# Reordering weight splits, activations and waits at the stage boundaries of a two-block fp32 kernel

## The reference

```python
h = h + jnp.concatenate([hm, ha], axis=-1) @ w_out[l]
h = h + memory_cross_attention(rmsnorm(h, g_cross[l]), rmsnorm(mem, g_mem[l]), ...)
h = h + peer_ffn(rmsnorm(h, g_ffn[l]), w_pq[l], ...)
```

## Time and profile before

| | |
|---|---|
| median of three executions | 1679.29 us (1677.75 to 1684.41) |
| profiled execution, its own time | 1677.7 us |
| its span, first to last instruction | 1675.9 us |
| busy: PE, DVE, ACT, POOL | 1652.3, 1237.3, 934.3, 237.0 us |
| DMA | 323.40 MB, mean 193 GB/s |

### The profile page before, as it was taken

The page is one execution under the profiler, slowest core; times in us unless marked ns, Lnnn a source line. Parts: engine busy times, 40 slices in busy tenths (PEclk is TensorE's granted clock), DMA queues, the critical chain, the costliest instruction groups (busy, mean ns, idle before and its releaser), DMA issues.

```text
span 1675.9 us, 30270 instructions
## 1 busy us (share of the span) xinstructions
PE 1652.3 (99%) x12006; PEld 1540.9 (92%) x12006; DVE 1237.3 (74%) x1894; ACT 934.3 (56%) x1138; POOL 237.0 (14%) x329
## 2 busy tenths in 40 slices
PE   8999999999999999999999999999999999999999
PEld 8899999999999999988888888999999888899987
DVE  6775467999998666666766767787799555769974
ACT  7875565545555555554554554786555357555542
POOL 0000000003757767301101000000000000000000
PEclk9999999999999999999999999999999999999999
DMA  8345244776555555777777776633555544345553
GB/s 303 129 158 190 103 179 139 227 235 216 186 177 189 189 189 189 270 238 241 237 243 237 240 244 220 232 127 126 184 198 198 190 163 151 126 152 202 202 186 116
DMA packets 73948, 323.40 MB, mean 193 GB/s; under 512 B 8679, under 2 KB 8935, under 8 KB 55888
## 3 DMA queue, kind: packets, MB, share of 16 engines
q1 hardware_dynamic: 58880, 285.18, 49.7%
q0 software_dynamic: 5568, 19.38, 3.8%
q10 hardware_dynamic: 9360, 16.92, 2.7%
HBM read 303.62 MB, written 17.83 MB: 192 GB/s over the span
## 4 chain that ended last, share of the span: by engine, by line
PE 82%; DVE 12%; ACT 4%; issue 1%; DMA 0%; SPq 0%; DVEq 0%; ACTq 0%
PE bank L598 13%; PE bank L599 13%; PE bank L600 13%; PE bank L980 7%; PE bank L979 7%; PE bank L981 7%; PE bank L932 5%; PE bank L935 5%; PE bank L936 5%; DVE lo_u L2261 3%; PE bank L944 2%; DVE wlo L1884 2%; DVE oh L2272 1%; ACT whi L1327 1%; DVE pos L2159 1%
## 5 line engine op out<-in xcount | busy, mean ns | idle before, releaser
L1561 ACT ACTIVATE hi_u<-raw_u 128x1024 fp32r<-128x1024 f32 x256 | 271.8, 1062 | 280.6 <-PE bank L979 165.1
L1884 DVE TENSOR_TENSOR wlo<-raw,whi 128x2048 fp32r<-128x2048 f32 x137 | 314.1, 2292 | 112.0 <-PE bank L598 84.8
L1327 ACT ACTIVATE whi<-raw 128x2048 fp32r<-128x2048 f32 x137 | 263.1, 1921 | 73.3 <-PE bank L598 70.5
L932 PE MATMUL bank<-xh,hi_u 128*128 128x256 f32 x1024 | 292.4, 286 | 1.3 <-DVE lo_u L2261 1.1
L2261 DVE TENSOR_TENSOR lo_u<-raw_u,hi_u 128x1024 fp32r<-128x1024 f32 x192 | 238.2, 1240 | 72.6 <-PE bank L932 63.3
L935 PE MATMUL bank<-xl,hi_u 128*128 128x256 f32 x1024 | 285.9, 279 | 0.0
L936 PE MATMUL bank<-xh,lo_u 128*128 128x256 f32 x1024 | 285.8, 279 | 0.0
L598 PE MATMUL bank<-nh,whi 128*128 128x256 f32 x904 | 251.7, 278 | 2.1 <-DVE wlo L1884 0.9
L600 PE MATMUL bank<-nh,wlo 128*128 128x256 f32 x904 | 250.3, 277 | 0.0
L599 PE MATMUL bank<-nl,whi 128*128 128x256 f32 x904 | 250.3, 277 | 0.0
L518 POOL TENSOR_SCALAR oh<-kept,sel_T 128x128 f32<-128x128 f32 x256 | 199.5, 795 | 253.8 <-ACT sel_T L1611 170.0
(11 more groups left out here) (410 smaller groups left out, 3355.2 us busy)
## 6 DMA issues: line engine op xcount, KB each, us to landing
raw<-in_weights SPq DMA_DIRECT2D x138, 1024.0 KB, 4.8
raw_u<-in_experts SPq DMA_DIRECT2D x256, 512.0 KB, 4.2
aside<-a_out ACTq DMA_DIRECT2D x64, 256.0 KB, 3.5
a_in<-aside POOLq DMA_DIRECT2D x64, 256.0 KB, 3.7
const<-in_const SPq DMA_DIRECT2D x1, 1409.0 KB, 8.8
const<-in_const POOLq DMA_DIRECT2D x1, 1409.0 KB, 6.1
h<-in_x SPq DMA_DIRECT2D x2, 512.0 KB, 4.8
raw<-in_weights SPq DMA_DIRECT2D x4, 256.0 KB, 6.1
```

The lines of the kernel that those rows point to most:

```text
L932: mm = pe.matmul(out, w[0][:, kp], xh[:, k, :], start=(k == 0), stop=False)
L1327: a(A(whi[:, n % HIGH, :], raw[:, n % RAW, :], ACT.Copy), S("weights_hi"))
L1561: a(A(hi_u[:, u % HIGH_U, :], raw_u[:, u % RAW_U, :], ACT.Copy), S("unit_high"))
L1884: v(V.tensor_tensor(wlo[:, n % LOW, :], raw[:, n % RAW, :], whi[:, n % HIGH, :].bitcast(F32), ALU.subtract), S("weights_split"))
```

## The change

Work is moved. The same matrix products are computed. In the GLA gate the gain multiplies og instead of the gate, on another engine.

1. Start: the identity (128 columns) is loaded alone, both halves of x directly after it, slot 0 in two halves instead of four quarters. The iota follows behind slot 2. ACT and DVE do the first norm quarter ahead of the first weight quarter.
2. First mixer: ACT does `split_hi(10)`, `values(1)` and the mLSTM exponentials before the window exponentials. The eight of token block 1 are no longer in two parts. The sigmoid goes behind the square root of the head norm, the square and `split_hi(13)` behind the first `wT` drain. DVE's `split_lo(11)`, `(12)`, `(14)` change places too.
3. Residual stages 1, 2 and 4: DVE's split of the second slot of the next stage moves ahead of the last `norm_lo`, in two halves around it.
4. Keys: the wait moves into `key_products`.
5. Experts' end: `split_lo(BEFORE)` in two halves, one ahead of each pair of additions. The transposes of norm 4 go three matmuls later.
6. Odd mixer's begin: PE starts the third slot with the products that need only `whi`. The mean square moves ahead of `split_lo`, `norm_hi(6, 0)` and `(6, 1)` ahead of two squares.
7. GLA's end: the gain of heads 2 and 3 on POOL, on og.

```diff
-            sp.dma_start(kept[:, :], t["const"][:, 0:N_KEPT])...
+            sp.dma_start(kept[:, 0:P], t["const"][:, 0:P])...
...
+            for half in range(2):
+                sp.dma_start(raw[:, 0, place], t["weights"][0][:, place])...
             weights(1)
             weights(2)
+            sp.dma_start(kept[:, P:], t["const"][:, P:N_KEPT]).then_inc(S("iota_loaded"), 16)
...
# POOL
+            pool.wait_ge(S("gla_means"), 1)
+            for hd in (2, 3):
+                for tb in range(TB):
+                    x = og[:, tb, hd * T:(hd + 1) * T]
+                    pool.tensor_tensor(x, x, row("gla"), ALU.mult).then_inc(S("gla_gained"), 1)
...
# PE
-            pe.wait_ge(S("keys_loaded"), 16)
             def key_products(tb, part):
+                pe.wait_ge(S("keys_loaded"), 16)
...
-                        if half + j == 2 and tb == 0:
+                        if half + j + tb == 3:
                             drained("peer", 0, 1)
...
-            odd(1, between=lambda: spread_roots(6))
+            pe.wait_ge(S("weights_hi"), n + 1)
+            for k in range(KD):
+                freeing(pe.matmul(bank[:, 0:T], x_hi[:, k, 0:P], w_hi[:, k, :], start=(k == 0), stop=False))
+                pe.matmul(bank[:, 0:T], x_lo[:, k, 0:P], w_hi[:, k, :], start=False, stop=False)
+            pe.wait_ge(S("weights_split"), n + 1)
+            for k in range(KD):
+                pe.matmul(bank[:, 0:T], x_hi[:, k, 0:P], w_lo[:, k, :], start=False, stop=(k == KD - 1))
+            spread_roots(6)
+            mm = product(bank[:, T:2 * T], (w_hi, w_lo), normed[6], 1)
...
# ACT
             split_hi(9)
+            split_hi(10)
+            values(1)
+            a(A(mE[:, :, :], mE[:, :, :], ACT.Exp, scale=-1.0), S("mlstm_exp"))
+            a(A(small[:, 80:88], mcol[:, 8:16], ACT.Exp), S("mlstm_exp"))
             act.wait_ge(S("window_max"), 1)
             a(A(small[:, 160:176], small[:, 160:176], ACT.Exp))
             window_exps(0, range(8))
-            a(A(mE[:, :, :], mE[:, :, :], ACT.Exp, scale=-1.0), S("mlstm_exp"))
-            a(A(small[:, 80:88], mcol[:, 8:16], ACT.Exp), S("mlstm_exp"))
-            values(1)
-            split_hi(10)
-            window_exps(1, range(3))
             output_gates(0)
             split_hi(11)
-            window_exps(1, range(3, 8))
+            window_exps(1, range(8))
             output_gates(1)
             split_hi(12)
-            a(A(mo[:, :, :], mo[:, :, :], ACT.Sigmoid), S("output_gated"))
...
             a(A(small[:, 184:192], small[:, 184:192], ACT.Sqrt), S("head_roots"))
+            a(A(mo[:, :, :], mo[:, :, :], ACT.Sigmoid), S("output_gated"))
+            split_hi(14)
...
# DVE
-                norm_lo(n, 3)
+                    norm_lo(n, 3)
+                else:
+                    split_lo(SLOT_OF[name] + 5, 0)
+                    norm_lo(n, 3)
+                    split_lo(SLOT_OF[name] + 5, 1)
...
-            split_lo(BEFORE)
             for half in range(2):
+                split_lo(BEFORE, half)
                 for tb in range(TB):
...
+            mean_squares(6)
             odd(1)
-            inv_root(6)
+            inv_root(6, False)
...
-            gained_gate(2)
             mix_lo("gT", 0, 0, 0)
             mix_lo("gT", 1, 0, 1)
-            through_gate(2)
-            gained_gate(3)
-            through_gate(3)
+            for hd in range(2, 4):
+                drained("odd", 8 + hd)
+                through_gate(hd)
```

More of the change, by code:

```diff
@@ L1197, in scaled_heads @@
                         close(mm)
-            odd(1, between=lambda: spread_roots(6))
+            n = SLOT_OF["odd"] + 2
+            pe.wait_ge(S("weights_hi"), n + 1)
+            w_hi, w_lo = [w.rearrange("p (k n) -> p k n", k=KD) for w in (whi[:, n % HIGH, :], wlo[:, n % LOW, :])]
+            bank = open_("odd", 1)
+            of = cur["b"]
+            x_hi, x_lo = normed[6]
+            for k in range(KD):
[6 more added lines that the diff above has]
+            mm = product(bank[:, T:2 * T], (w_hi, w_lo), normed[6], 1)
+            cur["b"] = of
+            close(mm)
+            free_slot()
             pe.wait_ge(S("walpha_loaded"), 16)
@@ L1472, in _ @@
                 drain(A(mnum[:, hd, :, :], bank[:, 0:2 * (P + 1)].rearrange("p (b d) -> p b d", b=2), ACT.Copy), "mout", hd)
-            a(A(msq[:, :, :, :], mnum[:, :, :, 0:P], ACT.Square), S("mlstm_squares"))
-            split_hi(13)
             for hd in range(8):
@@ L1735, in _ @@
             ffn(0)
+            for i in range(2):
+                norm_hi(6, i)
             for tb in range(TB):
@@ L1738, in _ @@
                 squares(h, tb, 0, 2)
-            for i in range(4):
+            for i in range(2, 4):
                 norm_hi(6, i)
@@ L2093, in _ @@
                   S("mlstm_out") if tb else None)
+            split_lo(14)
+            memory_keys(2)
             mix_lo("wout", 0, 4, None)
```

65 lines of the change are left out of this document (36 added, 29 removed).

## The result

The kernel after took **1668.64 us** (median of 10 executions, 1666.01 to 1674.28), the kernel before on the same chip 1677.88 (10 executions). The ratio is 0.9947, 95% interval 0.9936 to 0.9958. The kernel after was timed twice more with the experiments, and there the ratio was once 0.9972 (0.9961 to 0.9983; median 1672.77) and once 0.9946 (0.9930 to 0.9961; median 1668.83). Over all timings the 26 executions of after have median 1671.4 and mean 1670.8, the 82 of before 1678.1 and 1678.9. So the gain is 6.7 us by medians and 8.1 by means, 0.4 to 0.5%. The first ten had some luck: 6 of them lie in the lower of two groups of times, of the next ten 3.

A forecast was written before the change was run, and what follows sets the result against it. PE, busy 99% of the span, bounds the kernel; only its 23.6 us of waiting can be gained. Terms 0.25 + 3.6 + 2.1 + 1.3 + 1.8 + 0.6 = 9.65 us gave 1668.05 or 1669.6; forecast 1668.8, range 1664.5 to 1674.5.

The forecast's parts named there:

- Start, 0.25 gained: Slot 0: x's second half lands 0.8 us or more earlier, DVE's weight quarter takes 0.69; 0.25 us left.
- First mixer, 3.6: First mixer: ACT's new order ends PE's waits for slot 10 and `wS`; 3.6 us gained, ends 2.4 and 4.4.
- slot 10: 2.8, `wS`: 1.3, 0.85 back: First mixer: wait for slot 10 gone, 2.8 us; wait of 1.28 gone too; PE then waits 0.85 for `hmT`.
- rival (a): First mixer's second half is the limit, as with a drain per table switch; mixer gives 1.1, 1671.3 us; chance 0.17.
- Residual stages and keys, 2.1: Earlier splits and later key wait gain 0.65 us at `up0`, 0.65 at `up1`, 0.8 at `pq`; ends 1.0 and 2.4.
- Experts' end, 1.3: Experts' end: half the split ahead of the first additions removes PE's first wait; 1.3 us, ends 0.7 and 1.5.
- Odd mixer, 1.8: Odd mixer's begin: 16 high-half matmuls cover PE's wait, root ready by 1376.6; 1.8 us, ends 1.0 and 1.9.
- GLA's end, 0.6: GLA's end: DVE sheds two products to POOL, taken at 1.6 us each; 0.6 us gained, ends -1.2 and 0.7.
- Rival (d): GLA's end: slow POOL products hold og and PE; slower kernel from 5.3 us each, 1683.4 at 6.4; chance 0.03.
- Rival (c), the clock: The clock's fall at 56 to 64 us, 1.7 us lost, vanishes or another comes: 1667.1 or 1670.5; chance 0.08.
- Rival (b), experts' stage: Experts' stage: DVE or unit loads set its end, so 4.65 us gained ahead shrink by 4; 1672.8; chance 0.08.

The follow-up runs named there:

- experiment 3: The kernel after with the first slot's old order of loads, norm and weight quarters, only the identity's separate load kept; 1672.7 us, ratio 0.9971.
- before again: The kernel before, unchanged, profiled once more; the clock fell at 56 to 64 us as in its first profile.
- experiment 5: The kernel after with residual-stage halves, experts' end and GLA's end undone, and of the odd mixer's part only PE's order kept; 1672.1 us, ratio 0.9964.

## Why the prediction was right, step by step

The time of 1668.8 was met at 1668.64, and that is partly luck. Worked out with the distances taken out, the gain is 9.8 us (mean of three profiles against two, which differ by 1.2 among themselves) where the sum said 9.65. Two misses in it nearly cancel: the start brought nothing, the mixer 0.3 to 0.4 more than its term. The median over all timings, 1671.4, lies 2.6 above the forecast because half of the executions have a slow up0. Nothing in the prediction allowed for that. The times of before, 1677.75 to 1684.41, held the hint: the highest stood 5 us above the median, and I took no account of it.

- **Start, 0.25 gained: wrong.** PE's first product came 0.8 later than in before's first profile. The term that was too large is the 0.8 us or more for the 320 KB that no longer go ahead of x's second half: over fourteen profiles it is about 0.5, if anything (experiment 3). DVE's quarter between norm and PE was counted rightly, at 0.69. At the first spread the two starts are equal on average, 27.59 and 27.56. What a start gains or loses is handed on through the mixer.
- **First mixer, 3.6: mechanism right, size a little low.** Counted from the first spread to the first residual transposes (131.36 in before), it takes 104.4 and 104.5 us in the two of before, in which the clock fell. With the new order it takes 100.5 in four profiles in which the clock fell and 101.0 in a fifth, so it gains 3.9 mostly. Where the clock held it takes 100.1 to 100.5. The milestones came to within 0.6 us of those predicted: slot 10's low half 75.6 (76.2), `wT` drains 100.84 (100.9), sigmoid 104.73 (104.9), last mix of `hmT` 116.51 (116.6). Together with the start I had PE 3.85 us earlier behind it; against before's first profile it was 3.8, 3.2 and 4.0 in the three profiles. That is so near because the start's miss and the mixer's surplus cancel, and before again stood 0.84 later there. No clean split "slot 10: 2.8, `wS`: 1.3, 0.85 back" exists: the end is where DVE ends. The new wait for a bank behind `kxT` I did not see; it appears only in profiles in which the clock did not fall, and DVE's last mix ended no later for it. The table switches in succession (1.28 us each, 0.01 to 0.02 us after the instruction before) cost what the rows of before said. The drain that the Trainium skill adds to each switch (ScalarE: Activation LUTs, "What ACT_TABLE_LOAD costs") is not there, and rival (a) with it.
- **Residual stages and keys, 2.1: right.** 0.7 to 1.0 at `pq` (0.8), 0.6 at up1 (0.65), 0.4 to 0.6 at up0 (0.65).
- **Experts' end, 1.3: a little high.** 1.0. DVE's first two additions end as worked out, but PE closed the last bank about 0.3 us later than I had it: the last addition begins at 1044.14, 1049.9 on the scale of before, and the second transposes wait for it at 1044.93, 2.63 us behind the first.
- **Odd mixer, 1.8: mechanism right, 1.6.** The spread comes 2.8 us after the slot's begin, as said. That PE's order alone is worth nothing, I had expected wrongly in the experiment, not in the prediction, where "since the mean square comes earlier" is the condition.
- **GLA's end, 0.6: right, 0.5.** The size taken for POOL, 1.6 us a product, fits the sum but not the single one: 5.49 for four, 2.84 for the first and 0.92 for each other. The end at 1455.21 is far from where it is needed. Rival (d) was nowhere near.
- **Rival (c), the clock:** it fell in both profiles of before and in one of three of after, so it can fall or hold with the change. Over all fourteen profiles it fell in the three of before and of the mixer's order alone, and in four of the eleven of after and its variants; whether the change makes the fall rarer is open. The mixer swallowed about three quarters of the 1.7 us. The rival priced it at the full 1.7 and was wrong in that.
- **Rival (b), experts' stage:** steps there are those of trains of another value (215 products at 358 us and 119 at 386 at 113.4 where before had 117.8, together 1.5 us). Nothing was given back.

## What to carry to other kernels

Follow the chain of the engine that *ends* a stage (here DVE's in the mixer), not the waits one by one: PE's shorter waits and a clock that does not fall both ended at the same DVE instruction. A loss that delays that chain too, as at the start, is not covered by it and goes through to the end of the stage. Before taking a few tenths of a per cent for an effect, profile the same kernel twice and compare start distances in the long matmul trains; if they differ, subtract them, and compare the rests. A change whose steps were all right can come out 4 us off by that alone.

## What the runs showed of the hardware that I had not expected

- Trains of 256-column products with a weight load each run at 113.4 or 117.8 ns from start to start, at the full granted clock, over 45 to 960 products. The value holds through slots and PSUM banks. As a rule it changes only where another shape, a wait or transposes come between; in one or two trains of a profile it changes behind a single step of 121 or 122 ns with no idle time shown (before, 114.73 us, behind 49 of 144 products). About four trains of five have the same value in two executions, the rest change. What in the chip sets it, no run shows; a phase in which the train starts would fit the pattern of slow, slow, fast with constant slots, and is only argued.
- GpSimd's product of two inputs, 128 x 256 values in fp32, takes 0.92 us, and the first of four takes 2.84, in all ten profiles that have them, to 0.01 us. The mean of 1.37 describes none of them. The first begins while VectorE splits weights, a `tensor_tensor` from two SBUF tiles, and ends 0.6 us behind that split, which is not slowed. The one-hot tiles that GpSimd makes in the experts' stage say the same: 196 of 256 take 0.61 us on average, and each of the 60 that take 1.41 lies beside a `tensor_tensor` of VectorE from SBUF for over 0.8 us. So it looks as if GpSimd's instruction stands still while such a one of VectorE runs. No experiment moved it away.
- While GpSimd's other three ran, VectorE's `scalar_tensor_tensor` of the same size slowed down: the first four took 3.26 us, the next four, with GpSimd idle, 2.05 in the same profile, and in experiment 5 all eight took 0.49 each. So moving two products (1.4 us) off VectorE cost it 1.2 us in four later instructions. That lay under cover here.
- The Trainium skill (GPSIMD Engine Reference, "Engine selection") gives GpSimd about half of VectorE's rate for two inputs. The rows are not far from it: two of the shorter products, 1.84 us for 512 columns in two instructions, stand against 0.69 in one for VectorE's same product. That is 2.7 times, with a fixed part of each instruction in it that no row separates. The below 1 us that the prediction estimated for one product holds for three of the four.

```profile
1449.72 5.49 POOL L551 TENSOR_TENSOR og<-og,rows 128x256 f32<-128x256 f32 x4 [81.63 <-DVE small L2635]
...
1449.66 2.29 DVE L1914 TENSOR_TENSOR wlo<-raw,whi 128x2048 fp32r<-128x2048 f32 x1
...
1452.23 3.26 DVE L2612 SCALAR_TENSOR_TENSOR og<-og,small,ov 128x256 f32<-128x256 f32 x4
...
1459.68 2.05 DVE L2612 SCALAR_TENSOR_TENSOR og<-og,small,ov 128x256 f32<-128x256 f32 x4
```

The four products one by one, shortest, median and longest in ns:

```profile
L551 POOL TENSOR_TENSOR og<-og,rows x4: 915/920/2842, 1449.7 to 1454.3; 128x256 f32<-128x256 f32 x4
```

- The same 512 KB transfer of x, third or fourth of its queue, let PE begin with x's second half at 7.6 to 9.5 us over fourteen profiles.
